# Whole expert matrices as units of the weight buffer, in a decoder layer with a hierarchical mixture of experts

## The reference

```python
def hier_moe(h, wg_r, bg_r, we_r, be_r, w_gate, w_up, w_down):
    ...
    for grp in range(N_GROUPS):
        sl = slice(grp * EXPERTS_PER_GROUP, (grp + 1) * EXPERTS_PER_GROUP)
        hid = (jax.nn.silu(jnp.einsum("nd,edf->nef", hf, w_gate[sl]))
               * jnp.einsum("nd,edf->nef", hf, w_up[sl]))
        y = y + jnp.einsum("nef,efd->nd", hid * combine[:, sl, None], w_down[sl])
```

## Time and profile before

| | |
|---|---|
| three runs | 1446.07 us median (1442.35 to 1446.69) |
| the profiled execution | 1445.35 us, span 1443.6 us |
| PE busy | 1387.6 us, 96% |
| PEld busy | 1042.8 us |
| DVE, ACT, POOL busy | 734.1, 508.0, 139.2 us |
| full gate and up loads | 56 each, 1024 KB, median 22.0 and 24.2 us to landing |
| full down loads | 26, 2048 KB, 23.6 us to landing |
| mean granted clock of TensorE | 0.989 of 2.4 GHz |

### The profile page before, as it was taken

One profiled execution on the slowest core, in us unless ns is written; L12 is line 12 of the kernel. 1 busy time (PEld: TensorE's weight loads), 2 busy tenths in 40 slices (PEclk: granted clock), 3 DMA queues, 4 the chain that ended last, 5 costly groups with the idle time before them and its releaser, 6 DMA issues.

```text
span 1443.6 us, 27033 instructions
## 1 busy us (share of the span) xinstructions
PE 1387.6 (96%) x11565; PEld 1042.8 (72%) x11565; DVE 734.1 (51%) x1301; ACT 508.0 (35%) x880; POOL 139.2 (10%) x335
## 2 busy tenths in 40 slices
PE   7999999999999999999999999999999999999996
PEld 7998989889899998887889988874443333333432
DVE  4684947667567556545554344653332332223326
ACT  5553434334265555555353344421111110101103
POOL 8010010202100000000000000012011011010100
PEclk9999999999999999999999999999999999999999
DMA  7633432243394544438546517588999999999997
GB/s 228 206 118 119 126 119 92 95 130 115 119 329 143 175 157 137 174 122 286 175 141 210 174 59 242 178 347 308 419 423 423 425 424 421 423 423 425 424 407 265
DMA packets 150575, 350.99 MB, mean 243 GB/s; under 512 B 13536, under 2 KB 95034, under 8 KB 131898
## 3 DMA queue, kind: packets, MB, share of 16 engines
q1 hardware_dynamic: 150458, 349.30, 65.4%
HBM read 347.18 MB, written 2.10 MB: 242 GB/s over the span
## 4 chain that ended last, share of the span: by engine, by line
PE 86%; DMA 7%; DVE 4%; issue 2%; ACT 1%; DVEq 0%; POOL 0%; SPq 0%; POOLq 0%; ACTq 0%
PE banks L981 22%; PE banks L1589 14%; PE banks L1389 12%; PE banks L1629 6%; PE banks L937 6%; DMA expert_unit<-in_moe_w_down_dram 6%; PE banks L1454 5%; PE banks L1671 4%; PE banks L976 2%; PE banks L1478 1%; PE banks L1501 1%; PE banks L1161 1%; PE banks L1438 1%; PE banks L1400 1%; PE banks L1188 1%
## 5 line engine op out<-in xcount | busy, mean ns | idle before, releaser
L1589 PE MATMUL banks<-expert_unit,pair_entries 128*64 128x512 f32 x1024 | 242.0, 618 | 19.2 <-issue 16.8
L981 PE MATMUL banks<-hidden_lo_chunks,piece 128*128 128x256 f32 x920 | 260.2, 283 | 0.0
L1856 ACT CAST piece<-arena_fixed 128x1024 fp32r<-128x1024 f32 (+1 forms) x158 | 161.4, 1031 | 172.6 <-PE banks L981 136.4
L2301 DVE TENSOR_TENSOR piece<-arena_fixed,piece 128x1024 fp32r<-128x1024 f32 (+1 forms) x158 | 188.3, 1216 | 39.0 <-ACT piece L1856 38.5
L1589 PEld LDWEIGHTS banks<-expert_unit,pair_entries 128*64 128x64 f32 x1024 | 74.1, 141 | 157.1 <-issue 154.6
L981 PE MATMUL banks<-hidden_hi_high_chunks,piece 128*128 128x256 f32 x928 | 179.0, 291 | 1.5 <-DVE hidden_lo_chunks L2284 1.5
L981 PE MATMUL banks<-hidden_hi_low_chunks,piece 128*128 128x256 f32 x912 | 176.3, 291 | 0.2 <-DVE piece L2301 0.2
L981 PEld LDWEIGHTS banks<-hidden_lo_chunks,piece 128*128 128x128 f32 x920 | 176.1, 191 | 0.0
L2565 DVE TENSOR_TENSOR loop_split<-arena_fixed,loop_split 128x2048 fp32r<-128x2048 f32 x48 | 107.9, 2288 | 101.5 <-ACT loop_split L2034 101.5
L981 PEld LDWEIGHTS banks<-hidden_hi_high_chunks,piece 128*128 128x128 f32 x928 | 144.7, 192 | 6.5 <-issue 2.2
L2833 DVE TENSOR_TENSOR arena_phases<-arena_phases,banks 128x512 f32<-128x512 f32 x128 | 81.7, 681 | 130.0 <-PE banks L1671 130.0
(11 more groups left out here) (431 smaller groups left out, 2003.8 us busy)
## 6 DMA issues: line engine op xcount, KB each, us to landing
expert_unit<-in_moe_w_gate_dram SPq DMA_DIRECT2D x56, 1024.0 KB, 22.0
expert_unit<-in_moe_w_up_dram SPq DMA_DIRECT2D x56, 1024.0 KB, 24.2
expert_unit<-in_moe_w_down_dram SPq DMA_DIRECT2D x26, 2048.0 KB, 23.6
arena_fixed<-in_w_in_dram SPq DMA_DIRECT2D x22, 2048.0 KB, 8.9
arena_fixed<-in_wk_mem_dram SPq DMA_DIRECT2D x8, 2048.0 KB, 8.8
arena_fixed<-in_wv_mem_dram SPq DMA_DIRECT2D x8, 2048.0 KB, 8.4
arena_fixed<-in_w_out_dram SPq DMA_DIRECT2D x8, 2048.0 KB, 8.0
arena_fixed<-in_wq_mem_dram SPq DMA_DIRECT2D x8, 2048.0 KB, 8.6
```

Source lines behind the costliest of these rows:

```text
L981: mm = pe.matmul(b[:, half * T:half * T + T], w(w_)[:, k % 8, :], hidden_x(x_, c), start=c + t == 0 and n > 0, stop=c == NC - 1 and t == 2 ...
L1589: mm = pe.matmul(bank[b][o, :].rearrange("p (g n) -> p g n", g=2), hs_pair[:, c, o], gate_up_unit(i(e))[:, :, c % (NC // 2), :], start=c = ...
L1856: nc.scalar.copy(piece_half(p, 0), raw_piece(p)).then_inc(piece_hi, 1)
L2301: V.tensor_tensor(piece_half(p, 1), raw_piece(p), piece_half(p, 0).bitcast(F32), ALU.subtract)\
```

## The change

A unit now holds one whole matrix of one expert: kind 0 the gate matrix, kind 1 the up matrix, kind 2 the down matrix. Every full load is one transfer of 16384 contiguous bytes per partition, instead of two of 8192 for gate and up. A product passes 256 columns. A pair's work is in four halves `gate_up(p, kind, half)` of eight chunks; the gate and the up products write the two halves of the same bank. Pieces are half matrices: 8192 bytes per partition. TensorE's order for the first pairs, SyncE's order and the waits follow from that. ScalarE copies the first four chunks of pair 0 alone, after VectorE's two; VectorE starts its copies with the second group, and six small operations of the expert weights come later on it. GpSimd's copies for a pair wait for the up halves of the pair before.

```diff
         def gate_up_unit(i):
-            return expert_unit[i].rearrange("p (g c n) -> p g c n", g=2, n=FF)
+            return expert_unit[i].rearrange("p (c n) -> p c n", n=FF)
...
-        def halves_done(p, half):
-            return 2 * half + p + 1 if p < 2 else 2 * p + half + 1
+        first_order = ((0, 0, 0), (0, 1, 0), (1, 0, 0), (0, 0, 1), (0, 1, 1), (1, 1, 0), (1, 0, 1), (1, 1, 1))
+        def halves_done(p, kind, half):
+            return first_order.index((p, kind, half)) + 1 if p < 2 else 4 * p + 2 * kind + half + 1
 
         def filled(u):
-            return sum(64 if NSLOT <= v < NSLOT + 6 else 16 if v in down_units else 32
-                       for v in range(u % NSLOT, u + 1, NSLOT))
+            return sum(32 if NSLOT <= v < NSLOT + 6 else 16 for v in range(u % NSLOT, u + 1, NSLOT))
...
             def load_unit(expert, kind, i, full):
-                if kind < 2:
-                    for gu, src in enumerate((moe_w_gate, moe_w_up)):
-                        w = src[0, bass.ds(expert, 1)].rearrange("e (p c) n -> p (e c) n", p=P)
-                        sp.dma_start(gate_up_unit(i)[:, gu], w[:, kind * (NC // 2):kind * (NC // 2) + NC // 2, :])\
-                            .then_inc(full, 16)
-                else:
-                    w = moe_w_down[0, bass.ds(expert, 1)].rearrange("e (p c) n -> p (e c) n", p=P)
-                    sp.dma_start(down_unit(i), w).then_inc(full, 16)
+                w = (moe_w_gate, moe_w_up, moe_w_down)[kind][0, bass.ds(expert, 1)]
+                sp.dma_start((down_unit if kind == 2 else gate_up_unit)(i),
+                             w.rearrange("e (p c) n -> p (e c) n", p=P)).then_inc(full, 16)
...
+            def half_free(p, kind, half, reader):
+                sp.wait_ge(pe_gu, halves_done(*reader, half))
+                rows = NC if kind < 2 else FF // P
+                cs = slice(half * rows // 2, half * rows // 2 + rows // 2)
+                for e in range(2):
+                    i = unit_of(p, kind, e) % NSLOT
+                    w = (moe_w_gate, moe_w_up, moe_w_down)[kind][0, 2 * p + e].rearrange("(p c) n -> p c n", p=P)
+                    sp.dma_start((down_unit if kind == 2 else gate_up_unit)(i)[:, cs], w[:, cs]).then_inc(unit_full[i], 16)
...
-            chunk_half_free(1, 1, 1)
-            chunk_half_free(1, 2, 2)
-            chunk_half_free(2, 0, 3)
+            for half in range(2):
+                half_free(1, 1, half, (0, 0))
+                half_free(2, 0, half, (0, 1))
+                half_free(1, 2, half, (1, 0))
+            pair_free(2, 1)
             pair_free(3, 0)
-            pair_free(2, 1)
...
-            def gate_up_chunk(b, c, i):
+            def gate_up_chunk(b, c, kind, i):
                 for e in range(2):
                     o = slice(e * CAP, e * CAP + CAP)
-                    mm = pe.matmul(bank[b][o, :].rearrange("p (g n) -> p g n", g=2), hs_pair[:, c, o],
-                                   gate_up_unit(i(e))[:, :, c % (NC // 2), :], start=c == 0, stop=c == NC - 1)
+                    mm = pe.matmul(bank[b][o, kind * FF:kind * FF + FF], hs_pair[:, c, o], gate_up_unit(i(e))[:, c, :],
+                                   start=kind == 0 and c == 0, stop=kind == 1 and c == NC - 1)
...
+                elif half == 0 or p < 2:
                     for e in range(2):
-                        pe.wait_ge(unit_full[place(e)], filled(unit_of(p, half, e)))
+                        pe.wait_ge(unit_full[place(e)], filled(unit_of(p, kind, e)))
...
+                if p and kind == 0:
+                    pe.wait_ge(pool_pair, 2 * p + half - 1)
+                for c in range(half * NC // 2, half * NC // 2 + NC // 2):
+                    if p == 0 and kind == 0 and c % 4 == 0:
+                        pe.wait_ge(act_pair, c // 4 + 1)
+                        if c:
+                            pe.wait_ge(dve_pair, c // 4)
+                    mm = gate_up_chunk(p % 2, c, kind, place)
+                mm.then_inc(pe_gu, 1)
...
-            gate_up(0, 0)
-            gate_up(0, 1)
+            gate_up(0, 0, 0)
+            gate_up(0, 1, 0)
             gather(8)
             gather(9)
-            gate_up(1, 0)
-            gate_up(1, 1)
+            gate_up(1, 0, 0)
             for c in range(10, NC):
                 gather(c)
-            gate_up(0, 2)
+            gate_up(0, 0, 1)
             pair_slots(0)
-            gate_up(0, 3)
+            gate_up(0, 1, 1)
+            gate_up(1, 1, 0)
             pair_slots(1)
-            gate_up(1, 2)
             hidden_transposes(0)
-            gate_up(1, 3)
+            gate_up(1, 0, 1)
             down(0)
             scatter(0, 0)
             scatter(0, 1)
+            gate_up(1, 1, 1)
+            scatter(0, 2)
+            scatter(0, 3)
...
+                else:
+                    act.wait_ge(dve_hs, 2)
                 act.wait_ge(act_hs, 2 * q + 2)
-                o = slice(4 * q + 1, 4 * q + 4, 2)
+                o = slice(4 * q + 1, 4 * q + 4, 2) if q else slice(0, 4)
...
-            for q in range(4):
+            for q in range(1, 4):
                 gathered(q, first)
...
-                    pool.wait_ge(pe_gu, halves_done(p - 1, half))
+                    pool.wait_ge(pe_gu, halves_done(p - 1, 1, half))
```

More of the change, by code:

```diff
@@ L574, in decoder_layer @@
         pe_gu, pe_dq = sem("moe_gate_up_half"), sem("moe_down_quarter")
-        pe_first_gu = sem("moe_first_gate_up_quarters")
-        last_gate_up = [[sem(f"last_gate_up{k}_quarter{q}_full") for q in range(2)] for k in range(2)]
+        last_gate_up = [[sem(f"last_{k}_half{h}_full") for h in range(2)] for k in ("gate", "up")]
         last_down = [[sem(f"last_down{k}_quarter{q}_full") for q in range(4)] for k in range(2)]
@@ L823, in pair_free @@
                     load_expert(p, kind, e)
[L825 to L844, removed]
@@ L846, in last_gate_up_free @@
             def last_gate_up_free(kind):
                 p = NPAIR - 1
-                for quarter in range(2):
-                    c = NC // 4 * quarter
+                for half in range(2):
+                    cs = slice(half * NC // 2, half * NC // 2 + NC // 2)
                     for e in range(2):
-                        if quarter == 0:
+                        if half == 0:
                             unit_free(p, kind, e)
-                        for f in range(2):
-                            w = (moe_w_gate, moe_w_up)[f][0, 2 * p + e].rearrange("(p c) n -> p c n", p=P)
-                            sp.dma_start(gate_up_unit(unit_of(p, kind, e) % NSLOT)[:, f, c:c + NC // 4],
-                                         w[:, kind * (NC // 2) + c:kind * (NC // 2) + c + NC // 4, :])\
-                                .then_inc(last_gate_up[kind][quarter], 16)
+                        w = (moe_w_gate, moe_w_up)[kind][0, 2 * p + e].rearrange("(p c) n -> p c n", p=P)
+                        sp.dma_start(gate_up_unit(unit_of(p, kind, e) % NSLOT)[:, cs], w[:, cs])\
+                            .then_inc(last_gate_up[kind][half], 16)
@@ L1603, in gate_up @@
                     for e in range(2):
-                        pe.wait_ge(unit_full[place(e)], filled(unit_of(p, half, e)))
-                if p == 0:
-                    pe.wait_ge(act_pair, q + 1)
-                    pe.wait_ge(dve_pair, q + 1)
-                elif p == 1:
-                    pe.wait_ge(pool_pair, max(q, 1))
-                elif q % 2 == 0:
-                    pe.wait_ge(pool_pair, 2 * p + half)
-                for c in range(4 * q, 4 * q + 4):
-                    mm = gate_up_chunk(p % 2, c, place)
@@ L1733, in _ @@
             before, last = NPAIR - 2, NPAIR - 1
-            gate_up(last, 0)
+            gate_up(last, 0, 0)
             pair_slots(last)
             hidden_transposes(before)
-            for q in range(1, 4):
-                gate_up(last, q)
+            gate_up(last, 0, 1)
+            gate_up(last, 1, 0)
+            gate_up(last, 1, 1)
             late_down(before, 0)
@@ L2841, in _ @@
                      for tt in range(NT) for e in range(2)]
-            for q in range(4):
+            for q in range(1, 4):
                 gathered(q, first)
-                if q == 0:
+                if q == 1:
                     overflow()
-                if q == 1:
                     expert_weights()
@@ L2858, in outputs @@
                     add(p, f)
-            pair_slots(0)
-            pair_slots(1)
-            hidden(0)
-            hidden(1)
-            outputs(0)
-            for p in range(2, NPAIR):
+            for p in range(NPAIR):
                 pair_slots(p)
-                if p < NPAIR - 1:
+                if 0 < p < NPAIR - 1:
                     outputs(p - 1)
@@ L3075, in copied_pair @@
                     c0 = NC // 2 * half
-                    if p == 1 and half:
-                        pool.wait_ge(act_hs, 3 * NC // 8)
-                        pool.wait_ge(dve_hs, 3 * NC // 8)
```

(3 more changed lines are left out.)

69 lines of the change are left out of this document (27 added, 42 removed).

## The result

The changed kernel takes 1450.72 us (median of 7 runs, 1448.53 to 1453.43), the kernel before 1444.17 us in the runs beside it (7, 1442.35 to 1447.01). The ratio is 1.0044 with a 95% interval of 1.0035 to 1.0053: slower by 0.44%, some 6.4 us. The forecast was 1447 us and within 0.3%. The profiled execution after took 1450.85 us with a span of 1449.0 us, 5.4 us more than the span before.

A forecast was written before the change was run, and what follows sets the result against it. Transfers set the pace; the end is the full loads' start plus bytes over rate plus 59.5 us. +4.8 - 3.5 = +1.3 us on 1446.07 gave 1447.4, say 1447 us; own range 1443 to 1451, widened to 1439 to 1455.

The forecast's parts named there:

- Term 1: Full gate and up loads: 16384 instead of 8192 bytes per partition raise the transfer rate, 3.5 us less.
- Term 2: Start of the last stage: full loads begin at 1019 us, 4.8 us later than before.
- The gain at the first products: First expert products of pair 0: new split of copies lets the first refill issue 3.1 us sooner.
- the stop before U1a: TensorE, before the first half of pair 1's up products: waits 4.0 us until that whole up matrix has landed.
- the walk: Step-by-step timing of TensorE's new order in the first pairs, giving full loads from 1019 us.
- The fall of the clock: TensorE products right behind its wait for pair 1's up matrix: clock drops to 1.2 GHz, costing 1.7 us.
- Term 3: Gate and up products: same columns in twice the instructions of 256 columns, taken to cost nothing.
- rival 1: Gate and up products: 256 columns really cost 0.127 us an instruction, 1455 us; chance 0.14.
- rival 2: Start: dearer wait for pair 1's up matrix, longer slow clock and another at 975 us; 1449 to 1451 us; chance 0.17.
- rival 3: Start and loads: stop costs no clock, loads run at 431 GB/s; 1443 us, 1441 with sooner landing; chance 0.17.
- rival 4: Transfers cost by the piece, so half as many end 16.8 us of stops; 1427 us; chance 0.04.

## Why the prediction was off

The direction was right, and 1450.72 us lies within the forecast's own range of 1443 to 1451 us. But the forecast of 1447 us was 3.7 us too low, and "within 0.3%", to which the prediction gave 0.56, did not come: the change is 0.44%, which it gave 0.25. Nor is 0.3% what a measurement can tell here; the interval is 0.09% to either side.

**Term 1, the rate, was right**: -3.5 us predicted, 3.4 by the rates and 3.7 to 3.9 us by the time of the kernel with split loads.

**Term 2, the start, was right in mechanism and too small**: +4.8 us predicted, +6.2 measured from the same start of 1014.2 us. The gain at the first products was as said (G0a at 973.27 for 973.5 us, first refill at 976.99 for 977.7). The step that failed is the stop before U1a: "A group of 2.1 MB issued from 980.8 to 982.1 on idle transfer engines" was the wrong row to take U1b's landing from. The transfer engines were not idle at 992.6 us; D1a, whose refill starts at G1a's end (985.95 us) and which the walk leaves out, stood ahead. The stop became 6.0 instead of 4.0 us, and with U1b ahead of D1a it is 3.4. (The walk also gives G1a 3.6 us where its own 3.43 would end it at 986.2; that changes nothing here.) The fall of the clock behind it was near the prediction: 5.00 - 3.67 = 1.3 us for 1.7.

**Term 3, products of 256 columns, was mis-sized**: 0 predicted, 2.5 to 2.7 us measured alone. Its reason held for the products: 0.114 us an instruction is just above the 0.112 from which the prediction counted it wrong, but half of a product of 512 columns takes 0.112 in the same chain (3.58 us for 16), so a quarter grew by only 0.07 us, far from the 0.127 of rival 1. It looked at the products only. Twice the instructions also mean twice the code: at the end a fetch that meets the output stores costs 0.5 to 0.9 us, as the two kernels with a changed skipped block show.

The other 1.5 us lie between the first refill and the last stop: 0.3 us in the products ahead of the full loads, the rest among the loads. Their rate is 423 GB/s with and without halved products, but that is rounded. Queue 1 moved from 1021 to 1383 us (packets, MB), in the kernel before and then with halved products:

```profile
q1 hardware_dynamic: 17620, 152.95, 100.9%
q8 instruction: 12, 0.20, 0.2%
```

```profile
q1 hardware_dynamic: 17598, 152.69, 100.7%
q8 instruction: 19, 0.31, 0.3%
```

0.26 MB less are some 0.6 us at that rate. And the landings of one load spread wider over the transfer engines, while TensorE waits for the last: from the first to the last of the 16, for the last full load, 2.8 us before, 3.9 with halved products, 5.0 in the changed kernel. Size alone does not make it: the split loads of 8192 bytes still have 4.1 us, and the last full down loads, of 16384 bytes in all three kernels, have 3.3, 4.8 and 5.0, so it comes with the products of 256 columns. In the changed kernel too the piece up to the last stop is 1.7 us shorter and not 3.5. More fetches pass among the loads (19 against 12 above, and 19 in the changed kernel), but whether they cause the spread was not tried and stays open.

So 1.4 us of the miss are term 2's, and 2.5 to 2.7 are term 3's, nearly all outside TensorE's products: 6.2 - 3.4 + 2.7 = 5.5 us by the parts, where the two spans differ by 5.4.

**The rivals.** The time fell where rival 2 had put it (1449 to 1451 us), but by luck and not by its reasons: the stop before U1a was dearer by its length, with no fall of the clock at 973 us and no longer one behind it. Rivals 1, 3 and 4 are excluded by 0.114 us an instruction, by the stop with its slow products, and by 18.2 us of waits for up loads that are left between 1100 and 1400 us (16.8 us before).

## What to carry to other kernels

A unit that must be complete before its first half is read should stand as far behind its last refill in the order of work as that refill takes to land, here 7.5 to 10 us; what is queued behind that wait, here SyncE's next refill and so every load after it, moves with it. A landing time is taken from a row with the same things ahead on the transfer engines, not from one on idle engines. Where transfers set the pace, a gain in rate is easily spent by a late start, since a late start is paid once and in full.

## What was not expected of the hardware

Code that is skipped can cost time: with the skipped block shorter by 40 products the output stores landed in 2.2 instead of 3.1 us, with one instruction fetch of 16384 bytes less just ahead of them. And the length of a stop does not tell the clock behind it: 32 products took 5.36 us behind a stop of 3.39 us, 5.61 behind 5.12, 5.00 behind 6.01 and 6.49 behind 6.29 us. Stops before the change show the same.
